# The second half of each layer's last weight unit loaded in nine transfers instead of one

## The chip, the cores and the metric

The kernel runs on one core of a Trainium2 chip. The metric is the device time of one execution in microseconds. Engines are named as in the profile: PE is TensorE's matmul side and PEld its weight load, DVE is VectorE, ACT is ScalarE, POOL is GpSimd, and SP is the engine that issues every load and store here ("SPq" in the rows is its queue of DMA issues).

## The reference, cut to what matters

A trunk of two layers over 256 tokens of width 1024, all in float32. Each layer does two things:

```
x = x + Mixer(RMSNorm(x))                 # layer 0: retention and HGRN2; layer 1: stick-breaking and differential attention
x = x + MoE(RMSNorm(x))                   # 4 groups x 8 experts; top-1 group, then top-2 experts in it
expert(xb) = (silu(xb @ w_gate[e]) * (xb @ w_up[e])) @ w_down[e]      # w_gate, w_up: 1024 x 512; w_down: 512 x 1024
```

The output is x after layer 1. The weights of all 32 experts of both layers are read from HBM once: each of the three matrices of an expert is 2 MB.

## The kernel before, in words

**Units.** Weights come into a buffer of twelve places, each 128 partitions of 16 KB, which is 2 MB and is called a unit. A layer takes 8 or 6 units for its input projection, 2 for its output projection, and 96 for its experts. Units 16 to 83 of the experts are loaded four at a time by `load_matrices` (line 398, 8 MB a transfer, source `in_together`); the rest by `load_expert_unit` and `load_unit` (line 374, 2 MB a transfer).

**Experts in quads.** Four experts are worked on together, each in 32 of PE's 128 output rows. A quad takes 12 units: four of w_gate, four of w_up, four of w_down. For the last quad of a layer the units of w_up and w_down are not one expert each but a quarter of the rows of all four experts (`QUARTERED`, source `in_quarters`), so that PE can use each unit when it lands. The last of them, unit 95, is cut once more: its first half (columns 0 to 2047 of each partition, 1 MB) holds what output columns 0 to 511 need, and its second half what columns 512 to 1023 need. Line 384 issues the two halves one after the other, the first on the semaphore `half_landed`, the second on the semaphore of its place.

**The end of a layer on PE** is in the `pe.Else()` branch of `moe_pe`, which is the branch taken with these inputs: `up_and_down(7, last=True)`, then `last_half(0)` (line 683, eight matmuls, waits for `half_landed`), ACT's copy of the result to `y_sb` (line 748), `spread_half(0, tc)` twice (line 548, four matmuls, which wait for the copy and add the experts' rows back to the tokens), `last_half(1)` (line 683, waits for the second half), in layer 0 `first_turns` (line 875), ACT's second copy (line 751), `spread_half(1, tc)` twice, and DVE's four copies of the sums to x (line 821). In layer 1, SP then stores x (line 516). In layer 0 the next layer's input projection begins (`project_next`, line 1033), whose first unit is also loaded in two halves of 1 MB (line 448, the first on `in_half_landed`), followed by further units (line 374).

**The order of loads** is the order in which SP's program issues them. Before each issue SP waits for `unit_used` to say that the place is free. After the last unit of layer 0 the next loads are those of line 448, which wait for places that the last quad frees, then those of lines 374, 453 and 456 and, once x is finished, the constants of line 461.

Of the kernel before, what the change touches and what calls it, by code (L numbers as in the profile page):

```python
# [23 lines left out]
P = 128  # L24
# [17 lines left out]
TILE = 4  # L42
# [11 lines left out]
HALF = UNIT // 2  # L54
# [7 lines left out]
PER_QUAD = MATRICES * TILE  # L62
QUARTERED = ((0, 0), (QUADS - 1, 1), (QUADS - 1, 2))
TOGETHER = range(16, 84)
GROUPS = 6
OVER_BUFFERS = RING // 2
SCRATCH = 1024
# [74 lines left out]
def build(nc, t, where, const_width, stop_after=4):  # L142
    with ExitStack() as ctx:
# [3 lines left out]
        def sem(name):  # L147
            return ctx.enter_context(nc.semaphore(name))
# [100 lines left out]
        lbw = sb("lbw", [P, 4, HEADS])  # L249
        both_strips = sb("both_strips", [P, SCORES])[:, :]  # L250
        tables = [part(f"final{l}", sum(math.prod(shape) for _, shape in TABLES[l])) for l in range(2)]

        def table(l, wanted, names="abc"):
            at = 0
            for name, shape in TABLES[l]:
                if name == wanted:
# [9 lines left out]
        over_i = sb("over_i", [P, 2], I32)  # L266


        names = ["small_landed", "tables_landed", "sums_started", "in_half_landed", "begin_landed", "begin_second", "begin_third", "begin_fourth", "gains_landed", "xt_first_landed", "xt_second_landed", "xt_third_landed", "even_dims", "odd_dims", "gather_begun", "xT_begun", "half_landed", "x_first_landed", "x_second_landed", "first_landed", "pos_landed", "lb_landed", "masks0_landed", "masks_landed", "consts_landed", "filler_ready", "gain_landed", "gain_used", "unit_used", "stored",
                 "act_turn", "dve_turn", "rope_args", "rope_ready", "pos_ready",  # L270
                 "squares", "normed", "x_start_turned", "hT_first", "hT_second", "diag_ready", "row_done", "f_scaled", "q_scaled", "lb_in", "lb_exp",
                 "f_sig", "f_ready", "f_log", "cum_ready", "q_sig", "mid_in", "mid_exp", "level_in", "level_exp", "near_ready",
# [7 lines left out]
        S = {n: sem(n) for n in names}  # L280
        proj_used = [sem(f"proj_used{i}") for i in range(2)]
        unit_landed = [sem(f"unit_landed{i}") for i in range(RING + WIDE)]
# [8 lines left out]
        n_moe = QUADS * PER_QUAD  # L291
        in_turn = []
# [4 lines left out]
        def unit_base(layer):  # L297

            return layer * (UNITS_IN[0] + UNITS_OUT + n_moe)
# [4 lines left out]
        def unit_place(layer, n):  # L304

            l, m, place = in_turn[unit_base(layer) + n]
            assert (l, m) == (layer, n)
            return place

        def expert_unit(layer, u):  # L310

            return UNITS_IN[layer] + UNITS_OUT + u

        def unit_free(layer, n):

            place = unit_place(layer, n)
            return max((i + 1 for i in range(unit_base(layer) + n) if in_turn[i][2] == place), default=0)

        def past_first(layer, n):

            u = n - UNITS_IN[layer] - UNITS_OUT
            return u % TILE if u in TOGETHER else 0

        def unit_landings(layer, n):

            place = unit_place(layer, n)
            return 16 * sum(in_turn[i][2] == place and past_first(*in_turn[i][:2]) == 0 for i in range(unit_base(layer) + n + 1))

        def last_use(layer, place):

# [2 lines left out]
        def slot(layer, n):  # L333

            place = unit_place(layer, n)
            return ring[:, place, :] if place < RING else wide[:, (place - RING) * UNIT:(place - RING + 1) * UNIT]

        def group_buffer(b):

            return ring[:, 2 * b:2 * b + 2, :].rearrange("p u (h n) -> p (u h) n", n=HALF)  # L340

        def wait_unit(eng, layer, n):
            n -= past_first(layer, n)
            eng.wait_ge(unit_landed[unit_place(layer, n)], unit_landings(layer, n))
# [25 lines left out]
        def _(sp):  # L370
            def load_unit(layer, n, dst_cols, src):
                if unit_free(layer, n):
                    sp.wait_ge(S["unit_used"], unit_free(layer, n))
                sp.dma_start(dst_cols(slot(layer, n)), src).then_inc(unit_landed[unit_place(layer, n)], 16)

            def load_expert_unit(layer, u):

                quad, matrix, j = u // PER_QUAD, u // TILE % MATRICES, u % TILE
                w, rows = (("w_gate", KC), ("w_up", KC), ("w_down", FC))[matrix]
                if u == n_moe - 1:  # L380
                    n = expert_unit(layer, u)
                    sp.wait_ge(S["unit_used"], unit_free(layer, n))
                    for b, signal in enumerate((S["half_landed"], unit_landed[unit_place(layer, n)])):
                        sp.dma_start(slot(layer, n)[:, b * HALF:(b + 1) * HALF],
                                     t["quarters"][layer, 2, j, :, b * HALF:(b + 1) * HALF]).then_inc(signal, 16)
                elif (quad, matrix) in QUARTERED:
                    load_unit(layer, expert_unit(layer, u), lambda s: s, t["quarters"][layer, matrix, j])
                else:
                    src = t[w][layer, quad * TILE + j].rearrange("(p c) n -> p (c n)", c=rows)
                    load_unit(layer, expert_unit(layer, u), lambda s: s, src)  # L390

            def load_matrices(layer, u):

                n = expert_unit(layer, u)
                place = unit_place(layer, n)
                assert place % TILE == 0
                sp.wait_ge(S["unit_used"], max(unit_free(layer, n + j) for j in range(TILE)))
                sp.dma_start(places[:, place * UNIT:(place + TILE) * UNIT], t["together"][layer, u // TILE]).then_inc(
                    unit_landed[place], 16)

            def group_source(layer, quad, j):

                w, rows = (("w_gate", KC), ("w_up", KC), ("w_down", FC))[j // 2]
                part_ = slice((j % 2) * (rows // 2), (j % 2 + 1) * (rows // 2))
                src = t[w][layer, bass.ds(quad * TILE, TILE)].rearrange("e (p c) n -> p e c n", c=rows)[:, :, part_, :]
                return src.rearrange("p e c n -> p e (c n)")
# [36 lines left out]
            for layer in range(2):  # L443
# [22 lines left out]
                for u in FIRST_GATES[layer]:  # L466
                    load_expert_unit(layer, u)
# [3 lines left out]
                for u in (8, 9, 10, 11, 4, 5):  # L471
                    load_expert_unit(layer, u)
# [6 lines left out]
                for u in range(RING + WIDE, n_moe):  # L479
                    if u not in TOGETHER:  # L480
                        load_expert_unit(layer, u)
# [5 lines left out]
                with sp.If(count > SLOTS):  # L487
# [3 lines left out]
                    def over_group(n, quad, j):  # L491

                        if not (isinstance(n, int) and n == 0 and j < OVER_BUFFERS):
                            sp.wait_ge(m["used"], n * GROUPS + (j + 1 - OVER_BUFFERS))
                        sp.dma_start(group_buffer(j % OVER_BUFFERS), group_source(layer, quad, j)).then_inc(
                            over_landed[layer, j % OVER_BUFFERS], 16)

                    for j in range(GROUPS):
                        over_group(0, 0, j)
                    with sp.Fori(1, QUADS) as i:  # L500
                        for j in range(GROUPS):
                            over_group(i, i, j)
                    with sp.Fori(1, OVER_ROUNDS) as r:
                        with sp.Fori(0, QUADS) as i:
                            for j in range(GROUPS):
                                over_group(r * QUADS + i, i, j)
                    sp.wait_ge(m["used"], OVER_ROUNDS * QUADS * GROUPS)
                with sp.Else():
# [3 lines left out]
            for b in range(2):  # L512
                for tc in range(TC):
                    cols = slice(b * 512, (b + 1) * 512)
# [11 lines left out]
        def wait_matrices(eng, layer, rnd, i, matrices):  # L526
# [3 lines left out]
            else:  # L530
                eng.wait_ge(M[layer]["used"], (rnd - 1) * (QUADS * GROUPS) + i * GROUPS + 2 * matrices)

# [19 lines left out]
        def moe_pe(pe, layer, over, rnd):  # L552
# [121 lines left out]
            def last_half(n):  # L674

                if n == 0:
                    pe.wait_ge(S["half_landed"], 16 * (layer + 1))
                else:
                    wait_unit(pe, layer, expert_unit(layer, n_moe - 1))
                for e in range(TILE):  # L680
                    slots = slice(e * SLOTS, (e + 1) * SLOTS)
                    at = n * HALF + e * 512
                    mm = pe.matmul(psum[slots, YB + n, :], actT[:, FC - 1, slots],  # L683
                                   slot(layer, expert_unit(layer, n_moe - 1))[:, at:at + 512], start=False, stop=True)
                return mm
# [1239 lines left out]
def laid_out(inputs):  # L1925
# [23 lines left out]
    for l in range(2):  # L1949
        for u in TOGETHER:  # L1950
            w = inputs[("w_gate", "w_up", "w_down")[u // TILE % MATRICES]][l, u // PER_QUAD * TILE + u % TILE]
# [39 lines left out]
```

## Time and profile before

| | |
|---|---|
| median of three runs | 1174.34 us (1173.23 to 1175.51) |
| profiled execution, first to last instruction (its span) | 1174.3 us |
| profiled execution's own time | only its span is recorded |
| PE busy | 884.2 us, 75% of the span |
| DMA: mean over the span | 382 GB/s, 448.49 MB |
| chain that ended last | DMA 57%, PE 42% |

The span is that of the one execution that was traced. The median is of executions that were timed as a whole. Slices of the page are 29.4 us each. A digit in the DMA line is the mean busy share, in tenths, of the core's 16 DMA engines.

### The profile page before, as it was taken

The numbers are of one execution on the slowest core, as the hardware profiler recorded it, in microseconds if no ns is written. First come the engines' busy times: TensorE is split into PE (matmuls) and PEld (weight loads), VectorE is DVE, ScalarE is ACT, GpSimd is POOL, SyncE is SP. The second block draws the span as 40 slices with busy tenths as digits, with TensorE's granted clock in tenths as the row PEclk, the third lists the DMA queues.
The fourth block names the chain that finished last, engine by engine and source line by source line (L and its number), as shares of the span: only waits on it lengthen the run. The fifth ranks groups of instructions, "written<-read, shape, count | busy, mean of one in ns | idle before, by whom it ended". The sixth has DMA issues, their size and how long they took to land.

```text
span 1174.3 us, 11498 instructions
## 1 busy us (share of the span) xinstructions
PE 884.2 (75%) x5116; PEld 398.4 (34%) x5116; DVE 211.5 (18%) x438; ACT 143.1 (12%) x271; POOL 10.2 (1%) x11
## 2 busy tenths in 40 slices
PE   9999999748484747475899999977575747474776
PEld 7555554222121222221246655532121313131312
DVE  2732332000000010000026541410000000000001
ACT  3411311000000000000021431110000000000001
POOL 0000010000000000000000000000000000000000
PEclk9999999877787788888999999997777878888889
DMA  9771599999999999999996328999999999999997
GB/s 354 309 287 72 189 427 444 429 429 429 436 431 431 438 431 431 434 429 415 427 425 272 144 90 337 429 436 443 438 427 427 431 438 429 436 434 434 415 427 293
DMA packets 19635, 448.49 MB, mean 382 GB/s; under 512 B 2432, under 2 KB 2688, under 8 KB 5504
## 3 DMA queue, kind: packets, MB, share of 16 engines
q1 hardware_dynamic: 19584, 447.72, 89.8%
q8 instruction: 43, 0.70, 0.2%
q14 instruction: 8, 0.07, 0.0%
HBM read 446.66 MB, written 1.05 MB: 381 GB/s over the span
## 4 chain that ended last, share of the span: by engine, by line
DMA 57%; PE 42%; issue 0%; ACT 0%; SPq 0%; DVE 0%; DVEq 0%
DMA places<-in_together 48%; PE psum L614 13%; PE psum L992 11%; DMA places<-in_quarters 8%; PE psum L1093 5%; PE psum L989 4%; PE psum L1005 1%; PE psum L560 1%; PE psum L1033 1%; PE psum L548 1%; PE psum L541 1%; PE psum L1120 0%; DMA places<-in_w_in 0%; PE psum L536 0%; PE psum L683 0%
## 5 line engine op out<-in xcount | busy, mean ns | idle before, releaser
L614 PE MATMUL psum<-places,mixed 128*32 128x512 f32 x3040 | 424.1, 709 | 279.0 <-DMA places<-in_together 252.1
L614 PEld LDWEIGHTS psum<-places,mixed 128*32 128x32 f32 x3040 | 110.5, 128 | 573.7 <-issue 447.3
L992 PE MATMUL psum<-places 128*128 128x512 f32 x288 | 126.3, 593 | 0.0
L992 PEld LDWEIGHTS psum<-places 128*128 128x128 f32 x288 | 53.6, 190 | 61.4 <-issue 61.2
L560 PEld LDWEIGHTS psum<-sel,h 128*128 128x128 f32 x528 | 60.5, 192 | 17.0 <-issue 15.1
L560 PE MATMUL psum<-sel,h 128*128 128x128 f32 x528 | 64.3, 279 | 1.7 <-DVE sel L779 1.7
L803 DVE TENSOR_TENSOR mixed<-psum,sig 128x512 f32<-128x512 f32 x16 | 16.9, 1057 | 251.8 <-PE psum L614 251.8
L548 PE MATMUL psum<-y_sb,spread 128*128 128x512 f32 x128 | 59.6, 606 | 2.1 <-ACT y_sb L748 1.4
L734 ACT COPY mixed<-psum 128x512 f32<-128x512 f32 x34 | 19.7, 586 | 311.4 <-PE psum L560 311.4
L800 DVE TENSOR_TENSOR sig<-psum,sig 128x512 f32<-128x512 f32 x16 | 11.1, 692 | 250.6 <-ACT sig L739 250.6
L989 PE MATMUL psum<-places 128*128 128x256 f32 x192 | 42.9, 381 | 0.0
L809 DVE COPY y_sb<-psum 128x512 f32<-128x512 f32 x14 | 9.7, 692 | 179.6 <-PE psum L614 179.6
L739 ACT ACTIVATE sig<-psum 128x512 f32<-128x512 f32 x16 | 9.6, 597 | 254.1 <-PE psum L614 254.1
L989 PEld LDWEIGHTS psum<-places 128*128 128x128 f32 x192 | 36.1, 190 | 5.7 <-issue 1.0
L548 PEld LDWEIGHTS psum<-y_sb,spread 128*128 128x128 f32 x128 | 22.8, 189 | 38.6 <-issue 33.7
L748 ACT COPY y_sb<-psum 128x512 f32<-128x512 f32 x16 | 9.4, 585 | 210.9 <-PE psum L614 182.3
L1093 PE MATMUL psum<-places,y_sb 128*128 128x512 f32 x64 | 28.2, 594 | 0.7 <-ACT small L1372 0.7
L1093 PE MATMUL psum<-places 128*128 128x512 f32 x64 | 28.5, 592 | 0.0
L1364 ACT ACTIVATE places<-psum,small 128x512 f32<-128x512 f32 x16 | 10.1, 683 | 57.7 <-PE psum L992 53.6
L1005 PE MATMUL psum<-places 128*128 128x256 f32 x64 | 16.2, 419 | 1.2 <-DMA places<-in_w_in 1.2
L1093 PEld LDWEIGHTS psum<-places,y_sb 128*128 128x128 f32 x64 | 11.9, 190 | 14.8 <-issue 13.9
L1093 PEld LDWEIGHTS psum<-places 128*128 128x128 f32 x64 | 11.8, 190 | 13.4 <-issue 13.4
(261 smaller groups left out, 518.2 us busy)
## 6 DMA issues: line engine op xcount, KB each, us to landing
places<-in_quarters SPq DMA_DIRECT2D x22, 2048.0 KB, 35.6
places<-in_w_gate SPq DMA_DIRECT2D x16, 2048.0 KB, 26.4
places<-in_w_in SPq DMA_DIRECT2D x12, 2048.0 KB, 27.4
places<-in_w_down SPq DMA_DIRECT2D x8, 2048.0 KB, 15.8
places<-in_w_up SPq DMA_DIRECT2D x8, 2048.0 KB, 12.9
places<-in_w_out SPq DMA_DIRECT2D x4, 2048.0 KB, 14.2
places<-in_quarters SPq DMA_DIRECT2D x4, 1024.0 KB, 47.3
places<-in_w_in SPq DMA_DIRECT2D x2, 1024.0 KB, 29.3
```

The lines of the kernel that those rows point to most:

```text
L541: mm = pe.matmul(psum[:, ACC + b, :], ident, x[:, b % 2, (b // 2) * 512:(b // 2 + 1) * 512], start=True, stop=False, skip_group_check=True)
L548: mm = pe.matmul(psum[:, ACC + 2 * n + tc, :], spread[:, tc, :], y_sb[:, 512 * n:512 * (n + 1)], start=False, stop=False, skip_group_check ...
L560: mm = pe.matmul(psum[:, YB + c // 4 if bank is None else bank, (c % 4) * P:(c % 4 + 1) * P], h[:, tc, c, :], sel[:, tc, :], start=tc == 0 ...
L614: mm = pe.matmul(psum[slots, out + n, :], inp[:, c, slots], slot(layer, unit)[:, at + 512 * n:at + 512 * (n + 1)], start=c == 0, stop=c == ...
L734: nc.scalar.copy(xT[:, 4 * half:4 * half + 4, :], psum[:, YB + half, :].rearrange("p (c s) -> p c s", s=P)).then_inc(m["xT_ready"], 1)
L800: turn(nc.vector.tensor_tensor(sig, psum[:, GATE, :], sig, ALU.mult))
L803: nc.vector.tensor_tensor(act_h.rearrange("p c s -> p s c"), psum[:, UP, :].rearrange("p (s c) -> p s c", c=FC), sig.rearrange("p (s c) -> ...
L989: mm = pe.matmul(banks[:, m // 2, (m % 2) * SEQ:(m % 2 + 1) * SEQ], w[:, c, m * P:(m + 1) * P], hT[:, c, :], start=c == 0, stop=c == KC - 1)
L992: mm = pe.matmul(banks[:, m, :], hT[:, c, m * P:(m + 1) * P], w[:, c, :], start=c == 0, stop=c == KC - 1)
L1005: mm = pe.matmul(psum[:, 4 + m, 0:SEQ], w[:, c, m * P:(m + 1) * P], hT[:, c, :], start=c == 0, stop=c == KC - 1)
L1033: mm = pe.matmul(banks[:, m, :], hT[:, c, m * P:(m + 1) * P], w[:, c, :], start=c == 0, stop=c == KC - 1)
L1093: return pe.matmul(psum[:, OUT_BANK[layer] + 2 * tc + n, :], mixT(half)[:, c, tc * P:(tc + 1) * P], w[:, c, 512 * n:512 * (n + 1)], start= ...
```

## The change

The first half of unit 95 is issued as before (now by `load_rows`). The second half, 128 partitions of 8 KB, is issued as nine transfers: one of partitions 0 to 63 (512 KB), then eight of 8 partitions each (64 KB each), 64 to 71, 72 to 79, and so on to 127. All nine signal one new semaphore, `rest_landed`, and PE waits for 16 from each of the nine (144 in layer 0, 288 in layer 1) before `last_half(1)`. The second half of that unit no longer counts on the semaphore of its place, and `unit_landings` leaves it out. This is done in both layers. Sources, destinations and bytes are the same.

```diff
+EVEN_ROWS, FEW = 64, 8
+LAST_ROWS = [slice(0, EVEN_ROWS)] + [slice(p, p + FEW) for p in range(EVEN_ROWS, P, FEW)]
...
+        def own_signal(layer, n):
+
+            return n == expert_unit(layer, n_moe - 1)
+
         def unit_landings(layer, n):
 
             place = unit_place(layer, n)
-            return 16 * sum(in_turn[i][2] == place and past_first(*in_turn[i][:2]) == 0 for i in range(unit_base(layer) + n + 1))
+            return 16 * sum(in_turn[i][2] == place and past_first(*in_turn[i][:2]) == 0 and not own_signal(*in_turn[i][:2])
+                            for i in range(unit_base(layer) + n + 1))
...
                     sp.wait_ge(S["unit_used"], unit_free(layer, n))
-                    for b, signal in enumerate((S["half_landed"], unit_landed[unit_place(layer, n)])):
-                        sp.dma_start(slot(layer, n)[:, b * HALF:(b + 1) * HALF],
-                                     t["quarters"][layer, 2, j, :, b * HALF:(b + 1) * HALF]).then_inc(signal, 16)
+                    load_rows(layer, n, 0, slice(0, P), S["half_landed"])
+                    for rows in LAST_ROWS:
+                        load_rows(layer, n, 1, rows, S["rest_landed"])
...
+            def load_rows(layer, n, b, rows, signal):
+
+                cols = slice(b * HALF, (b + 1) * HALF)
+                sp.dma_start(slot(layer, n)[rows, cols], t["quarters"][layer, 2, TILE - 1, rows, cols]).then_inc(signal, 16)
...
                 if n == 0:
                     pe.wait_ge(S["half_landed"], 16 * (layer + 1))
                 else:
-                    wait_unit(pe, layer, expert_unit(layer, n_moe - 1))
+                    pe.wait_ge(S["rest_landed"], 16 * len(LAST_ROWS) * (layer + 1))
```

## Rows read from the trace of the kernel before

**Rows 1.** The page: DMA in 40 slices, and the chain that ended last.
```profile
DMA  9771599999999999999996328999999999999997
DMA 57%; PE 42%; issue 0%; ACT 0%; SPq 0%; DVE 0%; DVEq 0%
```

**Rows 2.** The chain in order of time, end of layer 1: start, us, what.
```profile
1116.98 46.66 DMA places<-in_quarters
1163.65 0.04 issue
1163.69 1.11 PE psum L683 x8
1164.80 0.02 issue
1164.82 0.59 ACT y_sb L748
1165.42 0.04 issue
1165.46 1.98 PE psum L548 x4
1167.44 1.04 PE psum L683 x8
...
1171.17 0.69 DVE places L821
```

**Rows 3.** PE in order of time, end of layer 0: start, us, ..., [idle before].
```profile
594.30 1.06 PE L683 MATMUL psum<-places,mixed 128*32 128x512 f32 x8 [0.36 <-DMA places<-in_quarters]
596.08 1.98 PE L548 MATMUL psum<-y_sb,spread 128*128 128x512 f32 x4 [0.71 <-ACT y_sb L748]
597.99 1.06 PE L683 MATMUL psum<-places,mixed 128*32 128x512 f32 x8
...
601.63 3.60 PE L1033 MATMUL psum<-places 128*128 128x512 f32 x8
```

**Rows 4.** Issue to landing, second half in layer 0 (started 547.2).
```profile
L384 SPq DMA_DIRECT2D places<-in_quarters x1: 9364/9364/9364, 547.2 to 547.2; - x1
...
DMA to landing us min/median/max: 49.5/49.5/49.5
```

**Rows 5.** The same, both halves in layer 1 (started 1117.0 and 1121.3).
```profile
L384 SPq DMA_DIRECT2D places<-in_quarters x2: 4230/4238/4247, 1117.0 to 1121.3; - x2
...
DMA to landing us min/median/max: 44.8/45.7/46.7
```

**Rows 6.** Windows at the end of layer 1; last columns: PEclk, DMA share, GB/s.
```profile
1150.00:1160.00 10.00, 6.93 (x40) 2.56 (x41) 0.66 (x2) 0.67 (x2) 0.00 (x0) 0.86 0.99 417
1160.00:1161.00 1.00, 1.00 (x5) 0.82 (x4) 0.00 (x0) 0.00 (x0) 0.00 (x0) 0.65 0.98 410
1161.00:1162.00 1.00, 1.00 (x11) 0.37 (x13) 0.00 (x0) 0.00 (x0) 0.00 (x0) 1.00 0.69 287
1162.00:1163.00 1.00, 1.00 (x16) 0.20 (x8) 0.00 (x0) 0.00 (x0) 0.00 (x0) 1.00 0.57 238
1163.00:1164.00 1.00, 0.71 (x8) 0.16 (x8) 0.00 (x0) 0.00 (x0) 0.00 (x0) 1.00 0.48 205
1164.00:1165.00 1.00, 0.76 (x8) 0.00 (x0) 0.00 (x0) 0.18 (x1) 0.00 (x0) 1.00 0.22 90
1165.00:1166.00 1.00, 0.54 (x2) 0.30 (x3) 0.00 (x0) 0.41 (x1) 0.00 (x0) 1.00 0.02 8
```

**Rows 7.** The window around the end of layer 0, same columns.
```profile
595.00:605.00 10.00, 9.29 (x36) 4.00 (x33) 4.06 (x6) 3.61 (x5) 0.00 (x0) 1.00 1.02 433
```

**Rows 8.** SP's issues in order of time, layer 0 to layer 1.
```profile
546.38 10.21 SPq L384 DMA_DIRECT2D places<-in_quarters  x2
571.01 0.81 SPq L448 DMA_DIRECT2D places<-in_w_in  x2
...
583.36 11.77 SPq L374 DMA_DIRECT2D places<-in_w_in  x2
602.55 0.33 SPq L461 DMA_DIRECT2D places<-in_consts  x1
```

**Rows 9.** Issue to landing, first half of layer 1's first unit (line 448).
```profile
L448 SPq DMA_DIRECT2D places<-in_w_in x1: 331/331/331, 571.0 to 571.0; - x1
...
DMA to landing us min/median/max: 28.2/28.2/28.2
```

More of the change, by code:

```diff
@@ L266, in build @@
         over_i = sb("over_i", [P, 2], I32)
-        names = ["small_landed", "tables_landed", "sums_started", "in_half_landed", "begin_landed", "begin_second", "begin_third", "begin_fourth", "gains_landed", "xt_first_landed", "xt_second_landed", "xt_third_landed", "even_dims", "odd_dims", "gather_begun", "xT_begun", "half_landed", "x_first_landed", "x_second_landed", "first_landed", "pos_landed", "lb_landed", "masks0_landed", "masks_landed", "consts_landed", "filler_ready", "gain_landed", "gain_used", "unit_used", "stored",
+        names = ["small_landed", "tables_landed", "sums_started", "in_half_landed", "begin_landed", "begin_second", "begin_third", "begin_fourth", "gains_landed", "xt_first_landed", "xt_second_landed", "xt_third_landed", "even_dims", "odd_dims", "gather_begun", "xT_begun", "half_landed", "rest_landed", "x_first_landed", "x_second_landed", "first_landed", "pos_landed", "lb_landed", "masks0_landed", "masks_landed", "consts_landed", "filler_ready", "gain_landed", "gain_used", "unit_used", "stored",
                  "act_turn", "dve_turn", "rope_args", "rope_ready", "pos_ready",
```

## The prediction

> **What bounds the kernel now.** I read the page first. In its 40 slices the DMA line stands at 9 almost throughout, and the chain that ended last is 57% DMA and 42% PE [rows 1]: for most of the span PE waits for weights. The change touches one megabyte per layer out of 448, so the averages say nothing about it. What decides is which wait ends last where a layer ends, and for that I went to the chain in order of time.
>
> At the end of layer 1 the chain runs through a DMA of 46.66 us that starts at 1116.98 and lands at 1163.64 [rows 2]. It is the issue at 1117.0, so it is the first half of the last unit, not the second. After it comes a rigid sequence: eight matmuls for the first half (1.11), ACT's copy (0.59), four matmuls that add the rows back (1.98), and only then, at 1167.44, the eight matmuls of the second half (1.04). They follow the previous matmuls with nothing between: the chain does not go to a DMA here. Layer 0 has the same picture. PE idles 0.36 us for a DMA before the first half at 594.30, and at 597.99 it starts on the second half with no idle time shown [rows 3].
>
> So the second half has slack, and its size follows from the issue rows. In layer 1 it is issued at 1121.3 and lands 44.8 us later, at 1166.1 [rows 5] (the smaller of the two landings is the later issue's: 1117.0 and 46.7 give the first half's 1163.7). PE comes to it at about 1167.4 [rows 2]: slack 1.3 us. In layer 0 it is issued at 547.2 and lands 49.5 us later, at 596.7 [rows 4]; PE comes at 597.99 [rows 3]: slack 1.3 us again. From first to second landing in layer 1 are 2.45 us, which is what 1 MiB takes at 430 GB/s (1.0486 MB / 430 = 2.44 us).
>
> The last view is the windows at the end of layer 1 [rows 6]. Until 1161 all 16 DMA engines are busy. Then the share falls to 0.69, 0.57, 0.48, 0.22, 0.02: about half of the engines are done with both halves by 1163, the others need up to 3 us more. Summed from 1161 that is 1.98 us of 16 engines; shared evenly, everything would have landed at 1163.0 instead of 1166.1. The engines are out of step, some 3 us from the early ones to the late ones.
>
> **The change part by part.**
>
> *What PE waits for.* The first half is issued first, with the same shape, the same bytes and the same place in the queue, and it is the one on the path. If a transfer's share waits in turn behind earlier ones on each DMA engine, its landing does not move: 0 us. Nothing in the change can give back more than PE's wait for the second half, and that wait is 0 in both layers.
>
> *Where the second half lands.* All transfers in the trace that matter here are of 128 partitions; none is of 8. So how the small ones are spread must be bounded. Lower bound: they fill exactly the idle time of the early engines, and the second half lands at 1163 to 1165 instead of 1166.1. Gain on the path: 0, since PE comes at 1167.4. Middle: each transfer of 8 partitions uses 8 engines, always the same ones. These carry a sixteenth of 512 KB and an eighth of 512 KB, 96 KB instead of 64, and take 1.5 x 2.44 = 3.66 us, 1.22 more than before; the others take 1.22 less. If the eight are the early engines, the second half lands at about 1166.1 - 1.2 = 1164.9. If they are the late ones, it lands at 1167.3 in layer 1 and 597.9 in layer 0, still within the slack of 1.3. Either way 0 us, with some 0.1 us a layer for being that close. Upper bound: the small transfers go one behind another at the pace of the partitions that they write (below, the first rival).
>
> The Trainium skill bears on this spreading ("DMA: Bandwidth & Descriptors", section on why a DMA increments its semaphore by 16): a transfer takes the largest number of engines up to 16 that divides its slowest dimension, and the lowest-numbered ones. That makes 8 engines for 8 partitions, the middle case. No row here shows a transfer of under 16 rows, nor which engines are the late ones; by this rule alone the sum stays 0.
>
> *SP's issues.* One issue becomes nine, in each layer. Unhindered an issue takes 0.33 us (331 ns on line 448, and 0.33 us on line 461) [rows 8, 9], so eight more are 2.6 us of SP. But the queue can be full: the second issue took 9.36 us in layer 0 and the two took 4.24 each in layer 1 [rows 4, 5], and SP got on only as earlier transfers drained. If SP has to wait before each of the eight until another 512 KB have drained (1.2 us at 430 GB/s, far more than its own 64 KB), SP is done at 556.6 + 10 = 567 in layer 0 and at 1125.5 + 10 = 1136 in layer 1. What stands behind it on SP: in layer 0 the loads of line 448, issued at 571.0 when PE frees their places [rows 8]; in layer 1 the stores at the very end. The margin is 4 us in layer 0. If that cover were gone it would still cost nothing soon: the transfer issued at 571.0 takes 28.2 us to land [rows 9], nearly all of it spent behind earlier data, so the issue could come 20 us later without the queue running dry. The constants of line 461 wait for x at 602.55, 7.4 us after SP is through with line 374 [rows 8]. Cost: 0.
>
> *What layer 1's first loads feel.* In layer 0 the queue does not end: the share is 1.02 from 595 to 605 [rows 7]. The eight engines that carry 32 KB more bring every later transfer to PE 1.22 us later if they are the late engines; if they are the early ones it comes up to 1.22 us sooner. The first half of the next projection lands at 571.0 + 28.2 = 599.2 [rows 9] and PE comes to it at 601.63 [rows 3]: slack 2.4 us, more than 1.22. Cost 0. From 600 on PE needs more time for a unit than its 2 MB need at 430 GB/s (4.9 us), so the slack grows.
>
> *PE.* One wait on a semaphore is exchanged for another, at the same point. Behind it on PE stand the eight matmuls of the second half, then all that remains of the layer; they feel it only if the landing passes 1167.4 or 598.0.
>
> **Sum.** 0 (first half) + 0.1 to 0.3 for two layers (second half near its limit) + 0 (SP) + 0 (next loads) = +0.2 us against the profiled span of 1174.3, which is the median of the runs (1174.34) within 0.04. Forecast: 1174.5 us, no change. A change of 0.2%, 2.35 us, is about what a measurement of this kernel can tell from none.
>
> **Rivals.**
>
> *The small transfers are slow because they write few partitions (slower).* In a transfer of 128 partitions each of the 16 engines serves 8 of them at 430 / 16 = 27 GB/s. If that is also what 8 partitions can take, a transfer of 64 KB to 8 partitions needs 2.4 us, eight of them in a row 19.5, and 512 KB to half the partitions 2.44 instead of 1.22. That is the far bound: 22 us instead of 2.44, less the slack of 1.3, +18 us a layer. The near bound is full overlap: the eight are issued ahead and write different partitions, so half of the partitions take 2.44 us after the other half took 2.44: 4.9 instead of 2.44, +1.2 us a layer after slack. It decides from the point where the second half needs more than 2.44 + 1.3 = 3.7 us. Since the engines are out of step they should spread over the partitions and come nearer to the overlap; I take +3 us a layer, 1180.5. For it: every large transfer in the trace goes to 128 partitions, so nothing shows that fewer are as fast. Against it: early engines start the second half 3 us ahead of the late ones, which pays for much of it. The Trainium skill states such a limit ("SBUF — State Buffer", "Door 1: The DMA port swizzle"): bandwidth follows the ports that the partitions reach, 64 partitions reach 8 of 16 and a block of 8 reaches two. By it the eight would take 1.2 us each in a row, 9.8 us, against 2.44 by the forecast; no run shown here tells. Chance 0.23.
>
> *The first half is held up (slower or the same).* Early engines, done with the first half, begin to write rows 64 to 127 while late engines still write their part of the first half to the same partitions. If they share, the first half lands later, by between 0 and the 2.44 us that a half of the unit takes; I take 0.8 a layer, 1176.1. For it: the 3 us between the engines [rows 6]. Against it: before, early engines also ran ahead, and nothing shows that they disturbed. It decides from 1.2 us a layer. Chance 0.15, of which 0.07 beyond the 0.2%.
>
> *The late engines are relieved and the first half lands sooner (faster).* If what makes them late is the traffic beside them, the first half could come up to 3.1 us sooner (1166.1 against the level 1163.0); taking half of that in both layers gives 1171.3. Against it: the first half is queued ahead of everything that changes. Chance 0.07.
>
> *The change does not do what it says*: a transfer of 8 partitions may be cut finer and use all 16 engines. Then engine loads stay as they were and the second half lands at 1166.1 as before: 1174.3, the same as the forecast on the clock. It shares its chance, 0.55 together.
>
> **How the numbers follow.** No change 0.55 (all within 0.2% but 0.02 on either side), first rival 0.23, second 0.15, third 0.07. Faster: 0.07 + 0.02 = 0.09. Slower: 0.23 + 0.07 + 0.02 = 0.32. Same: 0.59. The range must reach into the first rival: upwards to 1181, which leaves the serial cases out (0.1), downwards to 1172.5, which leaves most of the third rival out (0.06). The forecast's own range is 1173.2 to 1175.7.
>
> **What would show it.** If right: the chain after still goes through the first half's transfer, line 683 shows one wait for a DMA in each layer, about 0.3 us, and the second half's matmuls follow line 548 without a gap; the DMA share falls differently after 1161 but the first half lands 46 to 47 us after its issue. The first rival would show a second wait for a DMA at line 683, before the second half, of 1 us or more, and issues to landing of the last small transfers well past 45 us. The second would show the first half landing later against PE's last line 614 matmuls. The prediction is wrong if PE's gap before the second half is over about 1 us in either layer, or if SP is still issuing small transfers at 571.

## The result and the profile after

| | before | after |
|---|---|---|
| median | 1173.78 us (4 runs) | 1185.84 us (1184.86 to 1188.92, 4 runs) |
| ratio | | 1.0098, 95% interval 1.0083 to 1.0113 |
| span of the profiled execution | 1174.3 us | 1187.1 us |

The change costs 12 us, about 1%. The page hardly hints at it: PE is busy for 885.5 us instead of 884.2 and 448.49 MB are moved in both. The chain in order of time at the end of layer 1 does (start, us, what), against [rows 2]:

```profile
1121.39 46.73 DMA places<-in_quarters
1168.12 0.04 issue
1168.16 1.92 PE psum L626 x16
1170.09 3.53 another core or an unknown queue
1173.61 0.04 issue
1173.65 1.98 PE psum L695 x8
1175.63 0.02 issue
1175.66 0.59 ACT y_sb L760
1176.25 0.04 issue
1176.30 3.78 PE psum L560 x4
1180.08 1.19 PE psum L695 x8
1181.27 0.02 issue
...
1183.95 0.69 DVE places L833
```

The reader is to see four things. The transfer that lands at 1168.12 is unit 94, a whole unit issued just ahead of the first half; it took 46.7 us, where it took 45.2 before, and PE waited 3.15 us for it. The wait that ends at 1173.61 stands before the *first* half's matmuls (line 683 is now 695). The profile cannot name its transfer here, but the issue rows can, below. Third, between the first half's matmuls and the second's there is still no DMA: at 1180.08 they follow line 560 directly. Fourth, the same eight and four matmuls take 1.98 and 3.78 us where they took 1.11 and 1.98.

PE in order of time says the same of layer 0, against [rows 3]:

```profile
596.25 1.58 PE L695 MATMUL psum<-places,mixed 128*32 128x512 f32 x8 [2.93 <-DMA places<-in_quarters]
598.52 3.78 PE L560 MATMUL psum<-y_sb,spread 128*128 128x512 f32 x4 [0.69 <-ACT y_sb L760]
602.24 1.66 PE L695 MATMUL psum<-places,mixed 128*32 128x512 f32 x8
...
606.48 3.60 PE L1045 MATMUL psum<-places 128*128 128x512 f32 x8
```

Here PE idles 2.93 us before the first half instead of 0.36, and the next layer's projection starts at 606.48 instead of 601.63. The issue of the first half and its landing, layer 0 and layer 1, against [rows 4, 5]:

```profile
L402 SPq DMA_DIRECT2D places<-in_quarters x1: 433/433/433, 545.6 to 545.6; - x1
...
DMA to landing us min/median/max: 50.6/50.6/50.6
```

```profile
L402 SPq DMA_DIRECT2D places<-in_quarters x1: 1405/1405/1405, 1122.2 to 1122.2; - x1
...
DMA to landing us min/median/max: 51.4/51.4/51.4
```

1122.2 + 51.4 is 1173.6: the unnamed wait is for the first half. It takes 51.4 us instead of 46.7 in layer 1 and 50.6 instead of 47.9 in layer 0, although it is issued ahead of everything that was changed.

Windows at the end of layer 1 (last columns: PEclk, DMA share, GB/s), against [rows 6]:

```profile
1163.00:1164.00 1.00, 1.00 (x11) 0.50 (x4) 0.00 (x0) 0.00 (x0) 0.00 (x0) 1.00 1.06 369
1164.00:1165.00 1.00, 1.00 (x5) 0.55 (x3) 0.00 (x0) 0.00 (x0) 0.00 (x0) 1.00 1.05 221
1165.00:1166.00 1.00, 0.01 (x1) 0.00 (x0) 0.00 (x0) 0.00 (x0) 0.00 (x0) 1.00 0.80 172
1166.00:1168.00 2.00, 0.00 (x0) 0.00 (x0) 0.00 (x0) 0.00 (x0) 0.00 (x0) 1.00 0.92 221
1168.00:1170.00 2.00, 1.84 (x16) 0.42 (x16) 0.00 (x0) 0.00 (x0) 0.00 (x0) 1.00 0.88 188
1170.00:1172.00 2.00, 0.09 (x4) 0.00 (x0) 0.00 (x0) 0.00 (x0) 0.00 (x0) 1.00 0.52 111
1172.00:1174.00 2.00, 0.34 (x4) 0.20 (x8) 0.00 (x0) 0.00 (x0) 0.00 (x0) 0.88 0.09 37
1174.00:1176.00 2.00, 1.59 (x8) 0.00 (x0) 0.00 (x0) 0.34 (x1) 0.00 (x0) 0.50 0.06 25
```

This is the row to learn to read. Before, share and rate fell together: 0.48 went with 205 GB/s, and 0.48 x 430 is 206. Now, from 1164 to 1170, the share stays at 0.8 to 1.05 while the rate is 172 to 221. The engines are busy and move about half. A busy DMA engine is not one at its pace.

The trace also holds every packet, the piece of a transfer that one DMA engine moves at a time. A packet of 8 KB is one partition's row of a half unit, one of 16 KB a partition's row of a whole unit. Their median durations:

| stretch | 8 KB, us | 16 KB, us |
|---|---|---|
| before, 1157 to 1161.5 | 0.31 | 0.61 |
| changed, 1160 to 1163 | 0.31 | 0.61 |
| changed, 1164 to 1170 | 0.59 | 1.19 (4 packets, of unit 94) |
| changed, 1172 to 1178 | 0.31 | none |
| before, layer 0, 586 to 599 | 0.31 | 0.62 |
| changed, layer 0, 588 to 599 | 0.59 | 1.21 (5 packets, 588 to 590) |

So everything in flight goes at half pace, and it begins when the first engines turn to the second half. `half_landed` receives 16 updates for the first half, one for each engine's share. The first comes 42.0 us after the issue before and 41.8 after (at 1163.97), the last 46.7 and 51.4. Only the late engines are held up, and some of them still had packets of unit 94 to write. In layer 1 one engine alone is last: fifteen shares had landed after 48.6 us (45.9 before).

**Where the 12.8 us of the profiled execution are.** Layer 0: the first half takes 2.7 us longer, the work from its landing to the next projection 2.9 us longer (596.2 to 606.5, against 594.3 to 601.6), and it was issued 0.8 us earlier: 4.8 us in all. Layer 1: the first half 4.7 us longer, the work behind it 2.8 us longer (1173.6 to 1184.6, against 1163.7 to 1171.9). The remaining 0.4 us lie between.

### The profile page after: what moved, and what is told of

Read it like the earlier page. It is cut to its first block, busy times and chain, and to the rows that moved or that the text cites. A ratio compares the mean times of both kernels' runs of the same rounds, so it can differ in the third digit from the quotient of the medians.

```text
span 1187.1 us, 11514 instructions
## 1 busy us (share of the span) xinstructions
PE 885.5 (75%) x5116; PEld 398.6 (34%) x5116; DVE 211.5 (18%) x438; ACT 143.1 (12%) x271; POOL 10.2 (1%) x11
## 2 busy tenths in 40 slices
DMA packets 19763, 448.49 MB, mean 378 GB/s; under 512 B 2560, under 2 KB 2816, under 8 KB 5632
## 3 DMA queue, kind: packets, MB, share of 16 engines
HBM read 446.66 MB, written 1.05 MB: 377 GB/s over the span
## 4 chain that ended last, share of the span: by engine, by line
DMA 56%; PE 42%; another core or an unknown queue 1%; issue 0%; ACT 0%; DVE 0%; SPq 0%; DVEq 0%
DMA places<-in_together 47%; PE psum L626 13%; PE psum L1004 10%; DMA places<-in_quarters 8%; PE psum L1105 5%; PE psum L1001 4%; PE psum L1017 1%; PE psum L572 1%; PE psum L1045 1%; PE psum L560 1%; PE psum L553 1%; PE psum L695 1%; PE psum L1132 0%; PE psum L548 0%
## 5 line engine op out<-in xcount | busy, mean ns | idle before, releaser
L560 PE MATMUL psum<-y_sb,spread 128*128 128x512 f32 x128 | 63.2, 636 | 2.1 <-ACT y_sb L760 1.4
```

The source lines that it names most:

```text
L560: mm = pe.matmul(psum[:, ACC + 2 * n + tc, :], spread[:, tc, :], y_sb[:, 512 * n:512 * (n + 1)], start=False, stop=False, skip_group_check ...
```

## The experiments

Four theories stood from the trace. **A, crowding at the partitions written:** DMA engines that are done with the first half start on the second, write into few partitions, and so slow each other and the engines that still write the first half. **B, uneven engines:** eight engines carry 96 KB instead of 64. **C:** the number of issues, or the fuller queue. **D** is about PE: its matmuls after the wait run at the lower of its two clocks. Each ratio below is against the kernel before on the same chip. "First half" is its time from issue to landing in layer 0 and layer 1; before, 47.9 and 46.7 us.

| run | the second half's transfers | us | ratio, 95% interval | first half, us |
|---|---|---|---|---|
| (changed kernel) | 64 neighbours, 8 x 8 neighbours | 1185.84 | 1.0098, 1.0083 to 1.0113 | 50.6, 51.4 |
| e1 | 64 neighbours, 8 x 8 four apart | 1187.83 | 1.0097, 1.0075 to 1.0118 | 50.3, 50.8 |
| e2 | 64 neighbours, 4 x 16 neighbours | 1187.80 | 1.0090, 1.0061 to 1.0119 | 50.7, 51.2 |
| e3 | 0 to 63, 64 to 127 | 1184.28 | 1.0069, 1.0046 to 1.0092 | 51.3, 51.9 |
| e4 | even, odd | 1175.26 | 0.9998, 0.9988 to 1.0008 | 45.5, 47.6 |
| e5 | 64 to 127, 0 to 63 | 1185.80 | 1.0105, 1.0083 to 1.0128 | 51.6, 50.0 |
| e6 | 64 to 127, 8 x 8 of the lower | 1188.67 | 1.0114, 1.0096 to 1.0133 | 48.4, 51.1 |
| e9 | read blocks, write even and odd | 1174.15 | 0.9999, 0.9989 to 1.0009 | 47.3, 47.1 |
| e10 | read even and odd, write blocks | 1184.72 | 1.0085, 1.0061 to 1.0109 | 48.6, 51.9 |
| e13 | even, 8 x 8 of the odd | 1180.25 | 1.0043, 1.0029 to 1.0057 | 48.9, 48.8 |
| e14 | changed kernel again | 1187.90 | 1.0107, 1.0094 to 1.0120 | 52.2, 52.1 |
| e7 | as changed, PE kept busy | 1184.16 | 1.0084, 1.0067 to 1.0101 | 50.5, 51.4 |
| e15 | the same again | 1185.63 | 1.0086, 1.0072 to 1.0101 | 51.3, 50.4 |
| e11 | all 128, issued after the first half landed | 1176.65, one execution | none | 46.1, 46.9 |
| e16 | even, odd, issued likewise | 1177.55, one execution | none | 47.2, 46.5 |
| e12 | 0 to 63, 64 to 127, issued likewise | 1185.11, one execution | none | 45.2, 46.5 |
| e8 | as changed, issued likewise | 1197.92, one execution | none | 46.2, 47.6 |

**Which partitions are written together: e1 to e4.** Only one line of the changed kernel differs in each:

```diff
-LAST_ROWS = [slice(0, EVEN_ROWS)] + [slice(p, p + FEW) for p in range(EVEN_ROWS, P, FEW)]
+LAST_ROWS = [slice(0, EVEN_ROWS)] + [slice(p + i, p + i + 29, 4) for p in (64, 96) for i in range(4)]   # e1
+LAST_ROWS = [slice(0, EVEN_ROWS)] + [slice(p, p + 16) for p in range(EVEN_ROWS, P, 16)]                 # e2
+LAST_ROWS = [slice(0, 64), slice(64, P)]                                                                # e3
+LAST_ROWS = [slice(0, P, 2), slice(1, P, 2)]                                                            # e4
```

> The eight small transfers keep their number, their size and their 8 partitions each, but take every fourth partition (64, 68, ..., 92, then 65, 69, ... and so on) instead of eight neighbours. Theory A (the early engines write into the few partitions, or groups of them, that late engines are still writing, and crowd one another there): most of the loss goes, 1175 to 1180 us, and the first half lands under 49 us after its issue in both layers. Theory B (eight of the 16 engines carry 96 KB instead of 64 and are the late ones) and theory C (nine issues, or the fuller queue, hold the transfers up): no change against the changed kernel, 1184 to 1187.

> Partitions 64 to 127 as four transfers of 16 neighbouring partitions instead of eight of 8; five issues instead of nine. Theory A (crowding at the partitions written): still slow, 1179 to 1186, the first half 49 us or more from issue to landing. Theory B (eight engines carry more than the others): if 16 partitions go to 16 engines the load is even again, 1173 to 1176. Theory C (number of issues): about half of the loss, 1179 to 1181.

> The second half as two transfers of 64 neighbouring partitions each. Theory A (crowding at the partitions written): all engines turn first to partitions 0 to 63, so engines share there, the second half takes up to twice its 2.4 us, and the first half is held up by some of it: 1176 to 1182. Theories B and C (uneven load of engines, number of issues): like the kernel before, 1173 to 1175.

> The second half as two transfers of 64 partitions each, the even ones and the odd ones. Same number of transfers, bytes and rows per engine as with two neighbouring blocks of 64; only which partitions are written together differs. Theory A (crowding at the partitions written): like the kernel before, 1173 to 1175.5, and clearly less than with neighbouring blocks. Theory C (number of issues, or a transfer of 64 partitions is slow as such): the same as with neighbouring blocks.

e3 against e4 is the pair that tells. Both issue two transfers of 64 partitions and 512 KB; only which 64 differs. Neighbours cost 0.69%, every second partition nothing. So the loss needs neither nine issues nor small transfers nor an uneven load, and C and B are out as its main cause. A's ranges were too low, though: e2 (1187.80) and e3 (1184.28) both lie above them by about 2 us, and only the first half's 50.7 to 51.9 us are where A has them. e1 was a miss: spreading the small transfers over every fourth partition took nothing off, which says that the block of 64, issued ahead of them, does most of it, or that every fourth partition is no better than neighbours; e1 alone cannot tell these two apart.

Windows of e3, the columns as above:

```profile
1167.00:1168.00 1.00, 0.00 (x0) 0.00 (x0) 0.00 (x0) 0.00 (x0) 0.00 (x0) 1.00 1.05 262
1168.00:1169.00 1.00, 0.00 (x0) 0.00 (x0) 0.00 (x0) 0.00 (x0) 0.00 (x0) 1.00 0.97 205
```

and of e4, at the corresponding place:

```profile
1160.00:1161.00 1.00, 1.00 (x11) 0.37 (x13) 0.00 (x0) 0.00 (x0) 0.00 (x0) 1.00 0.61 254
1161.00:1162.00 1.00, 1.00 (x16) 0.20 (x8) 0.00 (x0) 0.00 (x0) 0.00 (x0) 1.00 0.51 213
```

In e3 a share of 0.97 moves 205 GB/s; in e4 half that share moves 213, as in the kernel before. The packets say the same: in e3 those of 8 KB take 0.59 us (1165.5 to 1172), in e4 0.31 throughout.

**Does it depend on which half comes first: e5, e6.** I thought that the early engines were those that write the upper partitions of a full transfer, so that the upper block first would leave each on its own ground.

```diff
+LAST_ROWS = [slice(64, P), slice(0, 64)]                                                                # e5
+LAST_ROWS = [slice(EVEN_ROWS, P)] + [slice(p, p + FEW) for p in range(0, EVEN_ROWS, FEW)]               # e6
```

> Two transfers of 64 neighbouring partitions as before, but 64 to 127 first and then 0 to 63. Theory A1 (crowding, and it comes about because the early engines are those that write the upper partitions of a full transfer: with 0 to 63 first they move onto partitions whose engines are late with the first half; with 64 to 127 first they stay on their own): the first half lands 46 to 48 us after its issue as in the kernel before, and the time is 1173 to 1177 instead of the 1184.3 of the other order. Theory A2 (a block of 64 partitions is slow as such, whichever it is): as slow as the other order, 1181 to 1187.

> The changed kernel mirrored: partitions 64 to 127 as one transfer, then 0 to 63 in eight transfers of 8. Nine issues, the same sizes. Theory A1: the first half is no longer held up (under 48.5 us from issue to landing) and the whole is within 3 us of the kernel before, 1173 to 1177; if the eight engines of the small transfers are the late ones, PE may wait up to 1 us for the second half. Theory A2 and theory C (number of issues): as slow as the changed kernel, 1183 to 1188.

Both came out no faster than their mirror images: 1.05% and 1.14%, against 0.69% and 0.98%. That theory of who gets in whose way fell. A block of 64 neighbours is slow whichever it is.

**Reading or writing: e9, e10.** So far source rows and destination partitions changed together. Here the rows are permuted in HBM, so that one side reads blocks while the other writes every second partition, and the reverse.

```diff
+LAST_ROWS, FROM_ROWS = [slice(0, P, 2), slice(1, P, 2)], [slice(0, 64), slice(64, P)]                   # e9
+LAST_ROWS, FROM_ROWS = [slice(0, 64), slice(64, P)], [slice(0, P, 2), slice(1, P, 2)]                   # e10
...
+                src = t["quarters"][layer, 2, TILE - 1, from_rows or rows, cols]
+                sp.dma_start(slot(layer, n)[rows, cols], src).then_inc(signal, 16)
```

> Two transfers of 64 rows that read two blocks of neighbouring rows in HBM (as in the slow two-halves run) and write the even and then the odd partitions (as in the harmless alternate run); the rows are permuted in HBM to fit. Theory A-dest (what matters is which partitions are written together): like the kernel before, 1173 to 1176. Theory A-source (reading a block of 512 KB from HBM with the pitch of 16 KB is what is slow): 1182 to 1187.

> The mirror: read every second row in HBM, write partitions 0 to 63 and then 64 to 127. Theory A-dest: slow like the two halves, 1182 to 1187. Theory A-source: like the kernel before, 1173 to 1176.

0.9999 and 1.0085: the written side decides, and the read side is worth nothing that can be measured. Packets of 8 KB took 0.31 us in e9 and 0.60 in e10 while the second half was written.

**The length by itself: e8, e11, e12, e16.** SP waits for the first half before it issues the second, so that no other load runs beside it at the end of layer 1. (The first stores of x run beside the last part of it in e12 and e8, from 1172.5 and 1180.5.)

```diff
                     load_rows(layer, n, 0, slice(0, P), S["half_landed"])
+                    sp.wait_ge(S["half_landed"], 16 * (layer + 1))
                     for rows in LAST_ROWS:
```

with `LAST_ROWS` of the changed kernel (e8), all 128 partitions (e11), two blocks (e12), and even and odd (e16).

> SP waits for the first half to land before it issues the nine transfers, so nothing of the second half can run ahead of the first. Theory A: the first half lands 46 to 48 us after its issue in both layers. The nine transfers then run alone; PE comes to them some 3.7 us after the first half, so it waits: 2 to 10 us in each layer, which is the length of the nine alone less 3.7. If the first half is still held up (50 us and more), something other than the second half's transfers does it. This kernel is slower by the wait, 1178 to 1192.

> The control of the nine that wait for the first half: one transfer of 128 partitions, issued by SP when the first half has landed. It runs alone. From the first half's landing to its own: 2.4 us of data and some 2 us around it, 4 to 5 us, against 11.5 us (layer 1) for the nine. Time 1176 to 1182.

> Two transfers of 64 neighbouring partitions, issued when the first half has landed. Theory A-dest with a rate that goes with the number of partitions written at a time: each takes as long as 128 partitions with twice the bytes, so 4.9 us of data and 2 around it, 6.5 to 7.5 us from the first half's landing. If a block of 64 is slow only beside other transfers: 4 to 5 us, as one transfer. Nothing runs beside it in layer 1.

> Two transfers, even and odd partitions, issued when the first half has landed. If the partitions written together decide, 4.5 to 5.5 us from the first half's landing to that of the second, as for one transfer; if it is the number of transfers or their size, 6.5 to 7.5 as for two blocks of 64.

The chain of e11 (one transfer), e12 (two blocks), e16 (even and odd) and e8 (nine), end of layer 1. In each the row of `places<-in_quarters` ends with the landing of the second half:

```profile
1162.84 5.04 DMA places<-in_quarters
1167.88 0.04 issue
```

```profile
1166.62 0.02 issue
1166.64 0.48 SPq L403
1167.12 0.06 issue
1167.17 7.35 DMA places<-in_quarters
```

```profile
1163.40 0.49 SPq L403
1163.89 0.06 issue
1163.95 4.80 DMA places<-in_quarters
```

```profile
1175.02 0.48 SPq L403
...
1178.12 8.37 DMA places<-in_quarters
```

From the first half's landing to the second's: 5.1 us for one transfer, 5.4 for even and odd, 7.9 for two blocks, 11.5 for the nine (1175.0 to 1186.5). Layer 0, with no stores but with the next layer's loads behind, gives 4.9, 5.2, 7.8 and 13.7. Two blocks cost 2.5 us more than even and odd (2.6 in layer 0), and 2.44 us is what 1 MiB takes at 430 GB/s: written in blocks of 64 neighbours, the same megabyte takes twice as long. The windows of e12 show it with nothing beside it:

```profile
1168.00:1170.00 2.00, 1.56 (x4) 0.68 (x4) 0.40 (x1) 0.38 (x1) 0.00 (x0) 1.00 1.03 238
1170.00:1172.00 2.00, 0.42 (x1) 0.00 (x0) 0.98 (x2) 0.00 (x0) 0.00 (x0) 1.00 1.05 229
```

All engines busy, 229 to 238 GB/s. Once under way a packet of 8 KB takes 0.31 us in e11 and e16, and 0.61 in e12. With eight small transfers in place of the second block it is another 3.6 us (11.5 - 7.9). That is not SP's issuing, which is over at 1178.4. The 64 packets of the small transfers run from 1178.6 to 1185.2, eight at a time, and from the second group on each takes about 0.81 us: one transfer after another, each on eight engines. The expectations for e11 and e12 were 0.1 and 0.4 us low and that for e16 held; e8's wait was in its range, but its 1197.92 us are 6 above the highest time expected. In e8 the first half landed after 46.2 and 47.6 us, as before: with nothing behind it, it is not held up. The second half's transfers do that.

**What the small transfers do alone: e13.**

```diff
+LAST_ROWS = [slice(0, P, 2)] + [slice(p, p + 15, 2) for p in range(1, P, 16)]                           # e13
```

> One transfer of the 64 even partitions (harmless as one of two, by the alternate run), then the odd ones in eight transfers of 8. If the loss of the changed kernel comes from the block of 64 neighbours: 1173 to 1176, first half 46 to 48.5 us from issue to landing. If the small transfers, each on a few partitions, do their own part (theory A-dest applied to them): the first half is still held up by 1 to 3 us a layer and the time is 1177 to 1184. If only the load of eight engines counts: the second half lands up to 1.2 us later, PE waits at most 0.5 us for it, 1174 to 1176.

With the 64 made harmless the loss is 0.43%, and the first half still lands late, at 48.9 and 48.8 us. So small transfers have a part of their own, about 5 us. In the trace of e13 PE is not slowed after the first half lands (line 560 takes 1.98 us). Its small transfers write every second partition, not eight neighbours, so this is no exact measure of the changed kernel's. Whether this part and that of the block simply add was not tried.

**PE's clock: e7, e14, e15.** Fillers (matmuls whose result is not used) keep PE busy while it waits. e14 is the changed kernel again, on the chip of e15.

```diff
-                            keep_busy(pe, 3, UP, ident, consts[:, 0:SEQ])
+                            keep_busy(pe, 3 if c == per else 8, UP, ident, consts[:, 0:SEQ])
...
                 if n == 0:
+                    keep_busy(pe, 6, UP, ident, consts[:, 0:SEQ])
                     pe.wait_ge(S["half_landed"], 16 * (layer + 1))
```

> The changed kernel, with filler matmuls on PE while it waits: 8 instead of 3 ahead of the last whole unit, and 6 ahead of the wait for the first half. Transfers are untouched. Theory D (about 6 of the 12 us are PE's matmuls after the wait at the lower of its two clocks, since it idled 3 us and more twice): 1178 to 1181, granted clock 1.00 after the first half lands, and the four matmuls that add the rows back take 2.0 us instead of 3.8. If the clock is no part of it: 1185 to 1188.

> The changed kernel once more, as the base for the fillers on the same chip: 1184 to 1188, ratio 1.008 to 1.011.

> The changed kernel with fillers on PE, as before. In the first profile the matmuls after the first half took 8.1 us in layer 1 as in the kernel before, instead of 11.0. If the clock is worth what the traces say, some 2.5 to 3 us in layer 1 and up to that in layer 0, less what PE then waits for the second half: 3 to 5 us under the changed kernel of the same call, 1180 to 1183. If it stays within 1 us of it, the clock's part is smaller than the traces say, or is given back at the second half.

e7: 1184.16 us, ratio 1.0084 (1.0067 to 1.0101), too near the changed kernel to tell and outside what was expected. e15: 1185.63 us, 1.0086 (1.0072 to 1.0101), against 1187.90 us of e14: 2.3 us less, under half of the 5.7 that the traces put on PE's path (below), again above the range expected, and the intervals still overlap, so that the times alone do not show a gain. In the trace of e15 the granted clock holds after the first half lands:

```profile
1174.00:1176.00 2.00, 1.29 (x9) 0.31 (x4) 0.00 (x0) 0.58 (x1) 0.00 (x0) 1.00 0.05 16
```

where the changed kernel's row of the same stretch has 0.50. From the first half's landing to the end it takes 8.4 us instead of 11.0 (8.2 before). In layer 0 only about 1.0 us of 2.9 comes back, since PE then comes to the second half before it has landed:

```profile
599.56 1.98 PE L560 MATMUL psum<-y_sb,spread 128*128 128x512 f32 x4 [0.71 <-ACT y_sb L761]
603.33 1.06 PE L696 MATMUL psum<-places,mixed 128*32 128x512 f32 x8 [1.79 <-DMA places<-in_quarters]
```

That is the second wait at this line that the first rival forecast. In the changed kernel it is hidden behind PE's own slower matmuls. (None of the variants beats the kernel before; e4 and e9 equal it.)

## Why the prediction was wrong

**The step that failed** is the first of the sum: "If a transfer's share waits in turn behind earlier ones on each DMA engine, its landing does not move: 0 us." The trace says nothing against the condition (the engine that is last lands its share of the first half at 1173.61, and nine more updates, one for each piece of the second, follow it up to 1177.21), but the conclusion does not follow. The engines are 3 us and more out of step, as [rows 6] showed, and what early ones write next slows what late ones still have to write: from 1164 packets of 8 KB take 0.59 us instead of 0.31, and unit 94's 1.19 instead of 0.61. Measured: 2.7 and 4.7 us in place of 0. e8 shows that it is the transfers behind that do it, e4 and e9 that it goes away when the same bytes are written to every second partition.

**The second rival named this mechanism and was undersized twice.** It bounded the delay by the 2.44 us of a half at full rate and took 0.8 us a layer, so that it hardly left "no change". The 4.7 us of layer 1 lie beyond its bound. The bound belonged at the slower pace that the first rival had worked out: at half rate one block of 64 alone takes 2.4 us instead of 1.2, and the small transfers are slower still. The two rivals were priced as alternatives, but the slow writing of the one is what holds up the first half in the other. The sign given for the second rival, a later landing of the first half, is what the trace shows. Neither sign that was named for the forecast being wrong came: PE has no gap before the second half, and SP is done at 564.9 in layer 0. The wait to watch was the one before the first half.

**The first rival** was right in its premise and wrong in its place. Writes to few partitions are slow: 7.9 and 11.5 us against 5.1 alone, that is 6.4 us more for the nine, between its near bound of 2.4 and its far one. Its "in a row" is right as well. Its sentence on the Trainium skill ("SBUF — State Buffer", "Door 1: The DMA port swizzle") was nearer to the chip than my choice: by it a block of 64 reaches half of the ports and goes at half rate, and by this case's runs it takes 2.5 us more per megabyte and goes at 229 to 238 GB/s. Every second partition reaches them all by the same table, and e4, e9 and e16 agree. For the small transfers the 9.8 us that it gave are too many: alone, in e8, the eight took 6.6 us in a row (1178.6 to 1185.2), 0.81 each instead of 1.2. But the place was wrong. PE never waits for the second half in the changed kernel: it lands at 600.8 and 1177.2, and PE comes to it at 602.2 and 1180.1, later than planned because of its own slowness. Had PE run at its old pace, it would have come at about 599.9 and 1177.3, too early in layer 0.

**What was not costed** is PE's clock. After idling 3.15 and 3.57 us at the end of layer 1, PE was granted 1.2 GHz instead of 2.4 (0.50 in the window 1174 to 1176), and the four matmuls of line 560 took 3.78 us instead of 1.98. From the first half's landing to the end that is 2.8 us in layer 1, and 2.9 in layer 0 to the next projection, 5.7 of the 12.8 us of the traced execution. The fillers gave back 2.3 us of the median and a part went into the next wait, so 5.7 is what the trace shows on the path, not what the clock alone would return. I priced a wait by its length alone.

**Two slips that change little.** The prediction set the traced span of 1174.3 us beside the median time of 1174.34, but a run's time is 1.8 us above its span (1188.92 and 1187.1 for the changed kernel's trace), so the traced execution before was a slower one than the median. And the third rival let the first half come up to 3.1 us sooner, a figure taken from the landing of the second (1166.1 - 1163.0).

**What held.** The slack of the second half and PE's lack of a wait for it. SP's issues: 545.6 + 19.3 is 564.9 in layer 0 (567 forecast) and 1122.2 + 18.7 is 1140.9 in layer 1, 18.7 us from the first issue where 19 were forecast, and both hidden. The "middle case" of eight engines with 96 KB: at the very end a share of 0.06, one engine of 16, moves 25 GB/s from 1174 to 1176, after the first half landed at 1173.6; at that pace 96 KB take 3.9 us, to about 1177.5, and the window after shows nothing moving from 1177. The updates of `rest_landed` confirm the eight engines: in each layer 8 come while SP issues the small transfers and 80 as data lands, 16 for the block and 8 for each small one; the last is at 1177.2. No cost came of it on the path, as said. That the next layer's loads were not felt was luck: the first half of its first unit landed at 603.1 (569.9 + 33.2) instead of 599.2, 3.9 us later where at most 1.22 was forecast. That is past the 601.6 at which PE came to it before, and is hidden only because PE now comes at 606.5.

```profile
1176.00:1177.00 1.00, 0.70 (x1) 0.50 (x2) 0.00 (x0) 0.24 (x1) 0.00 (x0) 0.50 0.04 16
1177.00:1178.00 1.00, 1.00 (x2) 0.34 (x1) 0.00 (x0) 0.00 (x0) 0.00 (x0) 0.50 0.00 0
```

**What stays open.** Which engines are the early ones and just whose writes meet whose: the order of the halves does not matter (e3, e5), which my picture of it would not give. Why one engine alone is 2.8 us behind the others with the first half in layer 1 (0.8 before). Whether e1 failed because of its block of 64 or its spacing; its packets of 8 KB take 0.56 us as soon as the block is begun (1164), which speaks for the block. How the parts of the block, the small transfers and the clock combine; the sums above are of one trace.

## What to carry to other kernels

Before splitting a load by partitions, ask which partitions the pieces write together: in this case a block of 64 neighbours went at half the rate of 128, every second partition at the full rate, and blocks of 8 neighbours one after another at a slower pace still (0.81 us a packet against 0.31). "It is queued behind" protects a transfer only if the engines are in step, so look in the windows for how far apart they finish, and price what comes behind as able to slow what is ahead. And price a new wait of PE with the matmuls behind it at the lower clock.

## What the runs showed of the hardware that was not expected

A transfer can slow one issued before it on the same queue: 51.4 us instead of 46.7 from issue to landing in layer 1, and 47.6 with nothing behind it. It even reached the unit ahead of that one, whose last 16 KB packets took 1.19 us instead of 0.61. Busy DMA share does not show such a loss; share times 430 GB/s, compared with the GB/s beside it, does: 0.97 with 205. And the pattern on the written side alone decides: 1.0085 against 0.9999 with the read side exchanged.
